# Output projection of a hybrid decoder block as seven half products of sums in place of eight

## What is computed

```
merged = (jax.nn.sigmoid(g_sb) * (o_sb @ w_branch_sb[l])
          + jax.nn.sigmoid(g_sa) * (o_sa @ w_branch_sa[l]))
x = x + merged @ w_out[l]
h2 = _rmsnorm(x, norm_mlp[l])
x = x + jnp.square(jax.nn.relu(h2 @ w_ff1[l])) @ w_ff2[l]
```

## Time and profile before

| | us |
|---|---|
| runs of the kernel, median of 3 (lowest, highest) | 725.2 (723.14, 725.34) |
| the profiled execution, its own time | 725.06 |
| its span from the first to the last instruction | 723.2 |
| PE busy | 715.8 |
| DVE, ACT, POOL busy | 536.8, 341.3, 261.5 |
| first matmul of the branch products | 300.33 |
| first matmul of the output projection | 343.86 |
| first matmul of the MLP | 389.98 |

### The profile page before, as it was taken

The page is one execution under the profiler, slowest core; times in us unless marked ns, Lnnn a source line. Parts: engine busy times, 40 slices in busy tenths (PEclk is TensorE's granted clock), DMA queues, the critical chain, the costliest instruction groups (busy, mean ns, idle before and its releaser), DMA issues.

```text
span 723.2 us, 9771 instructions
## 1 busy us (share of the span) xinstructions
PE 715.8 (99%) x3454; PEld 574.7 (79%) x3454; DVE 536.8 (74%) x771; ACT 341.3 (47%) x492; POOL 261.5 (36%) x207
## 2 busy tenths in 40 slices
PE   8999999999999999999999999999999999999997
PEld 5878878787777676788889978888888888888886
DVE  7355889899886876537746569695968779595897
ACT  6244753365567787722334353634344252634341
POOL 2005225011224563003300091815336180815586
PEclk9999999999999999999999999999999999999999
DMA  9309231311110301133290225151331505131103
GB/s 332 142 15 258 92 117 58 117 59 59 59 59 10 109 21 39 59 117 117 67 310 14 83 80 176 59 174 59 117 115 48 184 0 175 57 116 58 59 1 117
DMA packets 44039, 70.65 MB, mean 98 GB/s; under 512 B 2657, under 2 KB 27489, under 8 KB 44002
## 3 DMA queue, kind: packets, MB, share of 16 engines
q1 hardware_dynamic: 44000, 70.16, 29.4%
q10 hardware_dynamic: 2, 0.00, 0.0%
HBM read 65.71 MB, written 2.10 MB: 94 GB/s over the span
## 4 chain that ended last, share of the span: by engine, by line
PE 95%; DVE 2%; ACT 1%; POOL 1%; issue 1%; DMA 0%; DVEq 0%; ACTq 0%
PE ps L1950 8%; PE ps L1951 8%; PE ps L1952 8%; PE ps L1979 7%; PE ps L1980 7%; PE ps L1981 7%; PE ps L436 7%; PE ps L438 6%; PE ps L437 6%; PE ps L429 6%; PE ps L431 6%; PE ps L430 6%; PE ps L1861 1%; PE ps L1871 1%; PE ps L1755 1%; PE ps L1789 1%
## 5 line engine op out<-in xcount | busy, mean ns | idle before, releaser
L1950 PE MATMUL ps<-b_hi,cut_hi 128*128 128x512 f32 (+1 forms) x280 | 104.0, 371 | 0.0
L1951 PE MATMUL ps<-b_lo,cut_hi 128*128 128x512 f32 (+1 forms) x280 | 103.8, 371 | 0.0
L1952 PE MATMUL ps<-b_hi,cut_lo 128*128 128x512 f32 (+1 forms) x280 | 103.8, 371 | 0.0
L653 POOL TENSOR_TENSOR a_lo<-qo_sb,a_hi 128x512 fp32r<-128x512 f32 x56 | 93.9, 1700 | 14.2 <-ACT a_hi L976 14.2
L436 PE MATMUL ps<-cut_hi,a_hi 128*128 128x512 f32 x216 | 86.4, 400 | 0.0
L438 PE MATMUL ps<-cut_hi,a_lo 128*128 128x512 f32 x216 | 84.5, 391 | 0.0
L437 PE MATMUL ps<-cut_lo,a_hi 128*128 128x512 f32 x216 | 84.3, 390 | 0.0
L965 ACT ACTIVATE qo_sb<-ps 128x512 f32<-128x512 f32 x32 | 19.2, 599 | 130.2 <-PE ps L1952 84.0
L420 DVE TENSOR_TENSOR cut_lo<-raw,cut_hi 128x2048 fp32r<-128x2048 f32 (+2 forms) x33 | 51.2, 1551 | 28.0 <-ACT cut_hi L412 28.0
L661 POOL TENSOR_TENSOR qo_sb<-qo_sb 128x512 f32<-128x512 f32 x7 | 9.1, 1293 | 151.8 <-DVE qo_sb L1409 151.8
L412 ACT ACTIVATE cut_hi<-raw 128x2048 fp32r<-128x2048 f32 (+2 forms) x33 | 48.5, 1469 | 31.2 <-PE ps L431 22.7
(11 more groups left out here) (218 smaller groups left out, 1650.4 us busy)
## 6 DMA issues: line engine op xcount, KB each, us to landing
raw<-in_w_ff_dram SPq DMA_DIRECT2D x32, 1024.0 KB, 5.5
raw<-in_w_in_dram SPq DMA_DIRECT2D x16, 1024.0 KB, 5.4
gates<-in_x_dram SPq DMA_DIRECT2D x8, 512.0 KB, 5.7
raw<-in_w_out_dram SPq DMA_DIRECT2D x4, 1024.0 KB, 5.1
raw<-in_w_in_dram SPq DMA_DIRECT2D x4, 512.0 KB, 7.1
raw<-in_w_branch_sb_dram SPq DMA_DIRECT2D x2, 1024.0 KB, 5.1
raw<-in_w_branch_sa_dram SPq DMA_DIRECT2D x4, 512.0 KB, 6.3
out_dram<-gates SPq DMA_DIRECT2D x7, 256.0 KB, 2.8
```

The lines of the kernel that those rows point to most:

```text
L653: return pool.tensor_tensor(left_lo[:, q], left[q], left_hi[:, q].bitcast(F32), ALU.subtract).then_inc(l_lo, 1)
L1950: T.matmul(dst, w_hi[:, w], b_hi[:, k, a:b], start=(k == 0), stop=False)
L1951: T.matmul(dst, w_hi[:, w], b_lo[:, k, a:b], start=False, stop=False)
L1952: mm = T.matmul(dst, w_lo[:, w], b_hi[:, k, a:b], start=False, stop=(k == KD - 1))
```

## The change

merged is split into quarters (positions 0 to 255, called old, and 256 to 511, called new, by contraction rows 0 to 511 and 512 to 1023) and w_out into w11, w21, w12, w22. Seven products of 256 positions by 512 rows by 512 columns replace the eight. Left factors: m11 (A11), m12 (A12), m22 (A22) and four sums S3 = m11 - m21, S1 = m21 + m22, S2 = S1 - m11, S4 = m12 - S2. Right factors: w11, w21 (for A12), w22 (for S4) and four sums wt1 = w12 - w11 (S1), wt3 = w22 - w12 (S3), wt2 = w22 - wt1 (S2), wt4 = w21 - wt2 (A22). Here m11 and m12 are the new positions and m21 and m22 the old ones. Each product has two passes of 12 matmuls, t = 0 and 1. Products share banks and accumulate: A22 onto S3 in banks 2 and 3, S2 onto A11, S1 onto that and S4 onto that in banks 0 and 1, A12 in 6 and 7. In between DVE adds the bank to one part of x, and the next product into the bank waits until that addition has read it. The merged values go into `qo_sb`, not into `gates`. Six merges stay on POOL, two go to DVE; POOL makes S3, S1 and S4 and the low parts of all four sums, DVE makes S2 and the weight sums. The first MLP slabs, the residual and the gain are loaded in a new order, and the turn of tile 2 goes behind the first part of the MLP.

PE (the products in their order, and what each waits for):

```diff
+O_TURN = [O_A11, O_S3, O_A22, O_S2, O_S1, O_A12, O_S4]
+O_CUTS = [O_A11, O_S3, O_A22, O_S2, O_A12, O_S1, O_S4]
+O_BANK = {O_A11: 0, O_S2: 0, O_S1: 0, O_S4: 0, O_S3: 2, O_A22: 2, O_A12: 6}
+O_SUMS = [O_S3, O_S2, O_S1, O_S4]
+X_ADDS = [(O_S3, 0, 1), (O_A11, 2, 0), (O_A22, 0, 0), (O_S2, 0, 0), (O_S1, 0, 1), (O_A12, 2, 0), (O_S4, 2, 1)]
...
+            def out_product(q, turned=None):
+                w_hi, w_lo = o_home[q]
+                l_hi, l_lo = o_left[q]
+                pe.wait_ge(ow_lo, O_CUTS.index(q) + 1)
+                if q in O_SUMS:
+                    pe.wait_ge(os_lo, O_SUMS.index(q) + 1)
+                else:
+                    pe.wait_ge(mg_cut, 4 if q == O_A11 else 8)
+                opens = q in (O_A11, O_S3, O_A12)
+                for t in range(2):
+                    if q == O_A12:
+                        pe.wait_ge(br_out, 16)
+                    elif opens:
+                        pe.wait_ge(br_out, 12)
+                    else:
+                        pe.wait_ge(wo_out, added({O_A22: O_S3, O_S2: O_A11, O_S1: O_S2, O_S4: O_S1}[q]) - 1 + t)
...
+                    mm.then_inc(op_done, 1)
+                    if turned is not None:
+                        norm_turn(TB + turned[t], xn2[turned[t] % 2])
+
+            for q in O_TURN:
+                out_product(q, (0, 1) if q == O_A12 else None)
```

POOL:

```diff
+            for f in range(4):
+                merge(f)
+            pool.wait_ge(mg_sum, 4)
+            pool.tensor_tensor(osum[O_S3], m11, m21, ALU.subtract).then_inc(os_made, 1)
+            for f in range(4, POOL_MERGES):
+                merge(f)
+            out_sum_low(O_S3)
+            pool.wait_ge(mg_sum, POOL_MERGES)
+            pool.wait_ge(mg_late, KD - POOL_MERGES)
+            pool.tensor_tensor(osum[O_S1], m21, m22, ALU.add).then_inc(os_made, 1)
+            out_sum_low(O_S2)
+            out_sum_low(O_S1)
+            pool.wait_ge(os_made, 3)
+            pool.wait_ge(ow_lo, O_CUTS.index(O_A22) + 1)
+            pool.tensor_tensor(osum[O_S4], m12, osum[O_S2], ALU.subtract).then_inc(os_made, 1)
+            out_sum_low(O_S4)
```

DVE (gated(q, j) is the gating of bank j of round q; out_weight_low, merged_low are the low parts; the low parts of merged_low(0) to (3) are 256 positions wide):

```diff
+            out_weight_low(O_A11)
+            dve_cut(SL_BR + 2)
...
+            for j in range(4):
+                gated(0, j)
+            dve.wait_ge(*slab_arrived(SL_OUT + 2))
+            V.tensor_tensor(wt1, w12, w11, ALU.subtract).then_inc(ot_made, 1)
+            dve_cut(SL_BR + 3)
...
+            for j in range(4):
+                gated(1, j)
+            for j in range(3):
+                gated(2, j)
+            merged_low(0)
+            merged_low(1)
+            dve.wait_ge(*slab_arrived(SL_OUT + 3))
+            V.tensor_tensor(wt3, w22, w12, ALU.subtract).then_inc(ot_made, 1)
+            gated(2, 3)
+            merged_low(2)
+            merged_low(3)
+            dve.wait_ge(ot_made, 1)
+            V.tensor_tensor(wt2, w22, wt1, ALU.subtract).then_inc(ot_made, 1)
...
+            gated(3, 0)
...
+            V.tensor_tensor(wt4, w21, wt2, ALU.subtract).then_inc(ot_made, 1)
+            gated(3, 1)
+            out_weight_low(O_S3)
+            gated(3, 2)
+            gated(3, 3)
+            for f in range(POOL_MERGES, 8):
+                late_merge(f)
+            merged_low(4)
+            merged_low(5)
+            out_weight_low(O_A22)
+            merged_low(6)
+            merged_low(7)
+            dve.wait_ge(os_made, 2)
+            V.tensor_tensor(osum[O_S2], osum[O_S1], m11, ALU.subtract).then_inc(os_made, 1)
...
+            add_to_x(O_S3, 0)
+            add_to_x(O_S3, 1)
+            out_weight_low(O_S2)
+            for t in range(2):
+                add_to_x(O_A11, t)
+            add_to_x(O_A22, 0)
+            out_weight_low(O_A12)
+            add_to_x(O_A22, 1)
+            out_weight_low(O_S1)
+            for t in range(2):
+                add_to_x(O_S2, t)
+            out_weight_low(O_S4)
+            for t in range(2):
+                add_to_x(O_S1, t)
...
             second_scale(0)
+            add_to_x(O_A12, 0)
             second_scale(1)
             second_lo(0)
...
+            add_to_x(O_A12, 1)
+            f_low(0, 0)
+            second_lo(1)
+            add_to_x(O_S4, 0)
+            f_low(0, 1)
+            add_to_x(O_S4, 1)
```

SP:

```diff
+            sp.wait_ge(mg_sum, 4)
+            load_x(1)
+            sp.wait_ge(os_lo, O_SUMS.index(O_S3) + 1)
+            load_x(0)
...
+            sp.wait_ge(ow_lo, O_CUTS.index(O_S3) + 1)
+            load_w(0, 0)
+            sp.wait_ge(mg_sum, POOL_MERGES)
+            load_x(2)
+            sp.wait_ge(mg_late, KD - POOL_MERGES)
+            load_x(3)
+            sp.wait_ge(ow_lo, O_CUTS.index(O_A12) + 1)
+            load_f(0, 1)
+            sp.wait_ge(os_lo, O_SUMS.index(O_S1) + 1)
+            sp.dma_start(mlp_gain, norm_mlp.to_broadcast([P, D])).then_inc(mlp_gain_in, 16)
+            sp.wait_ge(ow_lo, O_CUTS.index(O_S1) + 1)
+            load_f(0, 0)
+            sp.wait_ge(ow_lo, O_CUTS.index(O_S4) + 1)
+            load_w(0, 1)
```

More of the change, by code:

```diff
@@ L200, in home_at, with four @@
             return late_home[g, q] if isinstance(g, int) and (g, q) in late_home else home[q]
+        merged = qo_sb
+        old, new = slice(0, 2 * P), slice(2 * P, S)
+        m11, m12, m21, m22 = (merged[:, a:a + 4, t] for t in (new, old) for a in (0, 4))
+        def four(t):
+            return t.rearrange("p (k t) -> p k t", k=4)
+        osum = {O_S3: four(slot(0, 2)), O_S1: four(slot(12, 2)), O_S2: four(slot(14, 2)), O_S4: four(slot(8, 2))}
+        b_flat = [t[:, :, :].rearrange("p a b -> p (a b)") for t in (b_hi, b_lo)]
+        o_left = {O_A11: [t[:, 0:4, new] for t in (a_hi, a_lo)], O_A12: [t[:, 4:8, new] for t in (a_hi, a_lo)],
+                  O_A22: [t[:, 4:8, old] for t in (a_hi, a_lo)], O_S3: [t[:, 0:4, old] for t in (a_hi, a_lo)],
+                  O_S1: [four(t[:, 4 * S:6 * S]) for t in b_flat], O_S2: [four(t[:, 6 * S:8 * S]) for t in b_flat],
+                  O_S4: [four(s4_parts[:, j, :]) for j in range(2)]}
+        w11, w21, w12, w22 = (raw[:, (SL_OUT + j) % RAW, :] for j in range(4))
+        wt1, wt3 = w11, w12
+        wt2 = qT_sa[:, :, :].rearrange("p a b -> p (a b)")
+        wt4 = slot(8, 4)
+        o_right = {O_A11: w11, O_S3: wt3, O_A22: wt4, O_S2: wt2, O_A12: w21, O_S1: wt1, O_S4: w22}
+        in_cut3 = (cut3_hi[:, :], cut3_lo[:, :])
+        in_cut = [(cut_hi[:, j, :], cut_lo[:, j, :]) for j in range(2)]
+        o_home = {O_A11: in_cut3, O_S3: in_cut[0], O_A22: [t[:, 0:4 * S] for t in b_flat], O_S2: in_cut3,
+                  O_A12: in_cut[1], O_S1: in_cut[0], O_S4: in_cut3}
         tok = [slot(0), slot(1)]
@@ L380, in slab_used @@
                 return gate_done, 2 * (i - SL_GATE) + 2
[L381 to L384, removed]
+            return br_done, 4 * (i - SL_BR) + 4
         def ff_arrived(j, g):
@@ L1351, in add_to_x, with out_weight_low @@
[L1351 to L1360, removed]
+            def out_weight_low(q):
+                dve.wait_ge(ow_hi, O_CUTS.index(q) + 1)
+                hi, lo = o_home[q]
+                V.tensor_tensor(lo, o_right[q], hi.bitcast(F32), ALU.subtract).then_inc(ow_lo, 1)
@@ new lines, in _, with add_to_x @@
+            out_weight_low(O_A22)
[3 more added lines that the diff above has]
+            V.tensor_tensor(osum[O_S2], osum[O_S1], m11, ALU.subtract).then_inc(os_made, 1)
+            def add_to_x(q, t):
+                n = [a for a, _, _ in X_ADDS].index(q)
+                m, half = X_ADDS[n][1] + t, X_ADDS[n][2]
+                dve.wait_ge(op_done, out_end(q) - 1 + t)
+                if q in (O_S3, O_A11):
+                    dve.wait_ge(x2_in[m], 16)
+                elif q != O_S4 and q != O_A22:
+                    dve.wait_ge(wo_out, added({O_S2: O_A22, O_S1: O_S3, O_A12: O_A11}[q]) - 1 + t)
+                part = xres[:, m, half * 512:(half + 1) * 512]
+                V.tensor_tensor(part, bank(O_BANK[q] + t), part, ALU.add).then_inc(wo_out, 1)
@@ L1911, in _ @@
                     mm.then_inc(br_done, 1)
[L1914 to L1921, removed]
-            slab_ready(SL_OUT)
```

209 lines of the change are left out of this document (114 added, 95 removed).

## The result

The changed kernel takes **728.28 us** (median of 4 runs, 728.09 to 728.60) where the kernel before took 724.21 in the same session (4 runs, 723.14 to 725.34): ratio 1.0061, 95% interval 1.0049 to 1.0073. That is slower by 4.1 us. The forecast was 729.1, range 719.8 to 732: plus 4.0 on a base of 725.1. With a fourth run the base is 724.2, so the added time came out closer (4.1 for 4.0) than the time itself.

A forecast was written before the change was run, and what follows sets the result against it. PE was taken to bound the kernel. Waits 1.2 + 4.3 + 0.2 + 3.3 = 9.0, plus 0.1 for each of four restarts, minus 5.44 gave plus 4.0 us: 725.06 to 729.1, range 719.8 to 732.

The forecast's parts named there:

- PE's own work: Output projection: 192 matmuls become 168, 24 fewer at 0.2267 us each, minus 5.44 us.
- The collision: DVE instructions with two SBUF inputs and POOL instructions never run together; a waiting 1024-column POOL operation costs DVE up to 2.23 us.
- first rival: The gain arrives: these forms do not collide, PE's waits fall to 0.4 us, time 720.0; chance 0.15.
- 4.9 us of waits: DVE's waits for POOL (0.5 + 2.2 + 2.2) in the queue ahead of S3's first addition to x.
- Waits: PE's losses in the projection: S3 1.2 us, A22 4.3, S2 0.2, S1 3.3, sum 9.0.
- restarts: PE starting again after each of four waits: 0.1 us each, an estimate from the longer matmul behind a turn.
- The tie at the port: At 360.8 DVE's and POOL's low parts for S2 come within 0.1 us; the winner moves up to 2.2 us.
- the layout: Queues laid side by side, each instruction at the later of its engine's last end and its semaphores; gives plus 4.0 us.
- bounds of plus 2 to plus 6: Around plus 4.0 us: durations 2 to 4% off give plus 3 to 5; port ties move up to 2.2 us.
- The clock's rival: Clock halves after PE idles before A22, swallowed by S1's wait; falling again before S1 adds 2.7 us: 731.8; chance 0.1.
- Late transfer: x tiles, w_ff slabs and gain go through SP in new order; x0 lands at 354.2, before its addition: hidden, nothing.
- The forecast of the MLP's start: The MLP, after the projection, starts at 393.2 without a wait, where before it began at 389.98.

The follow-up runs named there:

- experiment 10: Kernel before the change with 24 of the 192 matmuls of its output projection left out, all else as before: 719.68 us, ratio 0.9942.
- experiment 1: Changed kernel with POOL's three sums and four low parts replaced by zero fills that read nothing, all waits and DVE work kept: 719.75 us, ratio 0.9942.
- experiment 2: Changed kernel with DVE's four weight sums cut from 2048 columns to 64, POOL's work left as it is: 724.76 us, ratio 1.0013.
- experiment 3: Changed kernel with sixteen filler matmuls of zeros into unused bank 7 on PE in front of A22's waits: 730.85 us, ratio 1.0088.
- 7: Changed kernel with 16 filler matmuls before A22 and, on ScalarE, S4's weight high part ahead of S4's sum high part: 726.66 us, ratio 1.0036.
- experiment 9: Changed kernel with only ScalarE's swap, S4's weight high part ahead of S4's sum high part, no filler matmuls: 728.43 us, ratio 1.006.
- 8: Changed kernel with weight sums cut to 64 columns, plus 12 filler matmuls into bank 7 before the wait for S1: 722.45 us, ratio 0.9978.
- 4: Changed kernel with S3's two additions to x moved ahead in DVE's queue, around the low part of A22's weights: 731.49 us, ratio 1.0106.
- 6: Control: changed kernel's own orders, with waits written as in the kernel with new queue orders: 728.36 us, ratio 1.006.

## Why the prediction came out right

**PE's own work, minus 5.44.** Held in the projection (experiment 10, 5.4 from the trace). By medians of whole kernels it is between 4.0 and 5.4.

**The collision.** Held, and the loss needs it: without POOL's reads the kernel takes 719.75 (experiment 1), near the first rival's 720.0. It isn't enough by itself: with DVE's queue 7 us shorter the waits for S3 and A22 go, collisions or not (experiment 2), which is the prediction's own account, a full queue that holds 4.9 us of waits. Of six low parts of 2048 columns in the projection four had to wait for POOL, at 2.78, 4.30, 3.88 and 3.27 us where 3.3 to 4.5 were forecast, and two took 2.28; gatings didn't wait. (The price of a waiting POOL operation of 512 columns is written there as 1.12, 2.31 less 1.22; the difference is 1.09. The sum doesn't change.)

**Waits.** Each of the four terms, first as predicted and then from start to start: S3 1.2 and 1.23; A22 4.3 and 4.33; S2 0.2 and 1.62; S1 3.3 and 2.08. With 0.4 for restarts, 9.4 predicted and (with 0.13 up to the turn) 9.39 measured. The first two also hold in place: S3 at 350.25 (predicted 350.5), A22 at 360.02 (360.3).

**The last two are right only as a sum, and that by luck.** The tie at the port at 360.8 came at 360.4 and went to DVE, by 0.05 us (360.39 against 360.44), so S2 had no wait; the prediction had given it to POOL and had set its price at up to 2.2 us. The next low part, A12's, paid in its place (4.30). And the clock fell behind A22, to which the prediction gave a chance of 0.1. The sum fits, 1.62 + 2.08 = 3.70 where 0.2 + 3.3 + 0.2 for restarts were predicted, but out of two things that offset each other. With the tie at DVE and the clock at 1.00, experiments 3 and 7 lose only 1.36 us from A22 to S1 (12.24 less two products of 5.44). The tie alone, with the layout's own clock and nothing else new, would have made plus 1.7 of its plus 4.0, just below its bounds of plus 2 to plus 6; the fall of the clock put those 2.3 us back. The clock's rival said that the fall would be swallowed by the wait for S1. Of a longer fall that is shown (experiment 9); of the whole fall it isn't so, as the next paragraph has it. Where no later wait takes it up, a fall costs 1.6 us in the projection and 2.3 by the medians (experiments 2 and 8). No second fall came in front of S1.

**What the rival missed.** With PE kept busy, A22 to S1 takes 12.24 us (360.03 to 372.27 in experiment 3, 360.54 to 372.78 in 7) and not 14.6. A fall also delays A22's first addition (364.54 in the changed kernel; in experiment 3 it ends before 364.5), and by the rows that decides whether the low part of A12's weight gets to the port ahead of POOL. The two together were worth 1.8 us (728.43 in experiment 9, 726.66 in 7, on two chips; by the ratios, 1.006 and 1.0036, 1.7), and in experiment 3 the second path took it back. The 731.8 of that rival didn't come.

**Late transfer.** Nothing of the waits is a DMA's. The forecast of the MLP's start, 393.2, measured 392.86.

## What to carry to other kernels

When an algorithm trades matmuls for elementwise work, price the added work by the busiest queue and not by idle shares: DVE was idle for some 40% of both stages before, and yet 9.4 us were lost against 5.4 gained. Neither DVE's added work nor its waits for POOL did that alone: with POOL's reads gone PE waits 0.3 us, and with 7 us less in DVE's queue the first two waits go. Two-input work moved from DVE to POOL isn't off DVE's path if DVE has two-input work at the same time; giving part of it back to DVE and ordering each addition behind its product, both at once, turned plus 4.1 into minus 3.7 us. Lay the queues side by side before the change, and test the layout by removing the collision and by removing the load, in separate kernels.

## What the runs showed of the hardware that wasn't expected

- A POOL instruction that only writes doesn't hold up DVE's subtractions (experiment 1: the low part at 359.44 takes 2.28 us with POOL writing from 359.90; the four of 2048 columns take 9.6 us, and 14.2 beside POOL's subtractions).
- The clock fell behind waits of PE of 3.0 to 4.1 us (after, experiments 2, 3, 4, 6, 9), with fp32 matmuls of 512 columns 0.43 us apart instead of 0.2267: 1.9 times, not 2. It was still 1.00 behind those of 1.1 and 1.9 us (S3 and S1 in the changed kernel). In two kernels with the same wait it lasted 3.1 us (360.02 to 363.14) and over 5 (359.63 to 364.89).
- Who starts first goes first, by however little, and that shifts 2 us from one engine to the other: DVE by 0.05 us in the changed kernel (360.39 and 360.44; its low part 2.28 us), POOL by 0.24 us in experiment 2 (354.68 and 354.92; DVE's 4.32 us). The changed kernel's runs agreed within 0.5 us even so.
